# A recurrent mixer's instruction lists in another order, and the latent heads' key squares on another engine

## What is computed

```python
def wkv7_scan(r, w, k, v, a, b):
    # S_t = S_{t-1} diag(w_t) + (S_{t-1} a_t) b_t^T + v_t k_t^T ; y_t = S_t r_t
...
def rwkv7_mixer(r, k, v, dw, da, dg, w0, w2, a0, a2, g2, k_k, k_a, r_k, gn_w, gn_b):
    decay = jnp.exp(-jnp.exp(w_log))
    a = jax.nn.sigmoid((a0 + da @ a2).astype(f32))
    g = (jax.nn.sigmoid(dg) @ g2).astype(f32)
    kk = kk / jnp.maximum(jnp.sqrt(jnp.sum(kk * kk, axis=-1, keepdims=True)), 1e-12)
...
    y = wkv7_scan(rh, wh, kh, vh, -kk, kk * ah)
    y = ((y - mu) * lax.rsqrt(var + GN_EPS)).reshape(B, S, C) * gn_w + gn_b
    bonus = jnp.sum(rh * kh * r_k.astype(f32), axis=-1, keepdims=True) * vh
    return ((y + bonus.reshape(B, S, C)) * g).astype(r.dtype)
```

```python
    k_nope, v_mla = kv[..., :MLA_NOPE], kv[..., MLA_NOPE:]
    k = rms_norm_2(jnp.concatenate([k_nope, k_rope], axis=-1), g_mla_k)
    q = rms_norm_2(q, g_mla_q)
```

## Time and profile before

| what | us |
|---|---|
| median of 3 runs | 3263.35 (3263.17 to 3270.22) |
| the profiled execution | 3260.77 |
| its span, first to last instruction | 3258.7 |
| TensorE busy | 3138.0 (96%) |
| VectorE busy | 1681.2 (52%) |
| ScalarE busy | 1033.4 (32%) |
| GpSimd busy | 1968.5 (60%) |

### The profile page before, as it was taken

The page is one execution under the profiler, slowest core; times in us unless marked ns, Lnnn a source line. Parts: engine busy times, 40 slices in busy tenths (PEclk is TensorE's granted clock), DMA queues, the critical chain, the costliest instruction groups (busy, mean ns, idle before and its releaser), DMA issues.

```text
span 3258.7 us, 57483 instructions
## 1 busy us (share of the span) xinstructions
PE 3138.0 (96%) x20978; PEld 2472.2 (76%) x20978; DVE 1681.2 (52%) x2722; ACT 1033.4 (32%) x1860; POOL 1968.5 (60%) x2607
## 2 busy tenths in 40 slices
PE   7999999999999999999999999999999999999999
PEld 4767666678888886677778888877667778888887
DVE  4457777754553345525545644445551634555345
ACT  2153333321211113634443411123551536231112
POOL 4624333348688855254646888876336374898886
PEclk9999999999999999999999999999999999999999
DMA  5442111113233322022222333332113121333333
GB/s 213 143 161 60 42 41 47 41 54 117 69 97 97 99 74 71 27 66 65 65 66 72 91 97 97 97 92 83 40 35 90 45 84 46 94 94 97 97 97 97
DMA packets 70805, 265.42 MB, mean 81 GB/s; under 512 B 7744, under 2 KB 7872, under 8 KB 67520
## 3 DMA queue, kind: packets, MB, share of 16 engines
q1 hardware_dynamic: 68288, 257.59, 25.9%
q10 hardware_dynamic: 2304, 4.83, 0.4%
HBM read 260.29 MB, written 2.10 MB: 81 GB/s over the span
## 4 chain that ended last, share of the span: by engine, by line
PE 84%; DVE 9%; ACT 5%; issue 2%; DMA 1%; SPq 0%; DVEq 0%; ACTq 0%
PE psum_a L587 11%; PE psum_a L590 11%; PE psum_a L591 11%; PE psum_d L587 6%; PE psum_d L590 6%; PE psum_d L591 6%; PE psum_d L653 5%; PE psum_a L745 3%; PE psum_d L1119 2%; PE psum_d L848 2%; PE psum_a L775 2%; PE psum_a L779 2%; PE psum_a L778 2%; PE psum_a L616 1%; PE psum_a L619 1%
## 5 line engine op out<-in xcount | busy, mean ns | idle before, releaser
L3356 POOL TENSOR_TENSOR w_lo<-raw,w_hi 128x256 fp32r<-128x256 f32 x1736 | 1422.4, 850 | 36.2
L3350 POOL TENSOR_TENSOR mark<-mark 128x1 f32<-128x1 f32 x432 | 103.5, 240 | 1208.6 <-PE psum_a L587 610.8
L587 PE MATMUL psum_a<-h_hi,w_hi 128*128 128x512 f32 x1632 | 654.9, 401 | 6.2 <-ACT arena L1700 6.2
L591 PE MATMUL psum_a<-h_hi,w_lo 128*128 128x512 f32 x1632 | 636.9, 390 | 0.0
L590 PE MATMUL psum_a<-h_lo,w_hi 128*128 128x512 f32 x1632 | 636.9, 390 | 0.0
L3351 POOL TENSOR_SCALAR w_hi<-raw 128x1024 fp32r<-128x1024 f32 x434 | 460.9, 1062 | 33.1 <-DMA raw<-in_weights 33.1
L587 PEld LDWEIGHTS psum_a<-h_hi,w_hi 128*128 128x128 f32 x1632 | 306.6, 188 | 84.3 <-issue 11.0
L591 PEld LDWEIGHTS psum_a<-h_hi,w_lo 128*128 128x128 f32 x1632 | 306.8, 188 | 65.5
L590 PEld LDWEIGHTS psum_a<-h_lo,w_hi 128*128 128x128 f32 x1632 | 307.0, 188 | 61.5 <-issue 2.4
L587 PE MATMUL psum_d<-split,w_hi 128*128 128x512 f32 x848 | 329.9, 389 | 0.0
L590 PE MATMUL psum_d<-split,w_hi 128*128 128x512 f32 x848 | 329.9, 389 | 0.0
(11 more groups left out here) (374 smaller groups left out, 5272.9 us busy)
## 6 DMA issues: line engine op xcount, KB each, us to landing
raw<-in_weights SPq DMA_DIRECT2D x434, 512.0 KB, 3.6
plain<-in_ada SPq DMA_DIRECT2D x20, 1024.0 KB, 7.0
arena<-in_ada SPq DMA_DIRECT2D x4, 1024.0 KB, 16.8
x<-in_x SPq DMA_DIRECT2D x1, 2048.0 KB, 12.0
x<-in_x ACTq DMA_DIRECT2D x1, 2048.0 KB, 10.4
out<-x SPq DMA_DIRECT2D x8, 256.0 KB, 3.4
arena<-in_pe ACTq DMA_DIRECT2D x2, 512.0 KB, 3.8
const<-in_const ACTq DMA_DIRECT2D x1, 906.0 KB, 8.6
```

Of the source, the lines that this page charges most:

```text
L587: m = pe.eng.matmul(dst, wh, hi(t), start=t == 0, stop=False)
L591: m = pe.eng.matmul(dst, wl, hi(t), start=False, stop=t == k - 1)
L3350: eng.tensor_tensor(b.mark[:, 1:2], b.mark[:, 0:1], b.mark[:, 0:1], ALU.add)
L3356: m = eng.tensor_tensor(lo[:, part], b.raw[:, s, part], hi[:, part].bitcast(F32), ALU.subtract)
```

## The change

The mixer's lists:

- TensorE: `gate` is computed whole, ahead of the chain's maps (one tile of ring a in its turn, none taken ahead). The first of the pieces between the doublings has 4 weight tiles ahead of doubling 1 where it had 5, and 2 inside it where it had 1. The transposes of `R_KH` come behind the two products that follow them.
- ScalarE: the gate's Sigmoid comes ahead of the copies of the chain's outputs. `act_rwkv_decays` moves from doubling 2 to doubling 3, between the copy of the shifted input and `act_rwkv_length`.
- VectorE: the reciprocal of the group norm's deviation is two of 256 columns instead of one of 512, and it moves, with the first step of the norm behind it (`dve_rwkv_normed`), from behind `t_ready` to around the transitions, so ahead of the gate and the bonus. `dve_rwkv_mixed` moves from doubling 3 to behind `t_ready`. The steps of the next turn's inputs are dealt to other doublings: the scan (step 1) from the end of doubling 1 to that of 2, the first reciprocal from the end of 4 to the middle of 5 and the second from the middle of 5 to behind the maps.

The latent heads: the sums of the keys' squares are issued behind the first `uq` and ahead of the other three. ScalarE copies the upper half of a key bank and VectorE the lower half, then ScalarE squares all 128 rows from PSUM; VectorE's four squares go. The root of the key sums stands behind the first query.

```diff
 def pe_rwkv(pe, j, chain):
-    gate = PePieces(pe, "gate", 2 if chain else 0)
-    gate.part(4)
+    pe_features(pe, "a", "gate", H)
     if chain:
         chain.maps()
-    gate.part(4)
...
-    piece.part(5)
+    piece.part(4)
...
-        piece.part(1 if k == 1 else 2)
+        piece.part(2)
...
-    for src in (b.R_V, b.R_BH, b.R_KH):
-        turned = pe_turned(pe, [src[:, q * P:(q + 1) * P] for q in range(NQ)])
+    for src in (b.R_V, b.R_BH):
+        pe_turned(pe, [src[:, q * P:(q + 1) * P] for q in range(NQ)])
     pe_units(pe, "d", (B, R))
     maps = pe_units(pe, "d", (K, lambda v, row, out: AR[ROWS[row], 2 * v + out]), width=P)
+    turned = pe_turned(pe, [b.R_KH[:, q * P:(q + 1) * P] for q in range(NQ)])
 def pe_mla_heads(pe, half):
-        pe_features(pe, "a", "uk", of(b.s_hi, b.s_lo, 2), 1)
-    tiles = [pe_features(pe, "a", "uq", of(b.s_hi, b.s_lo), 2) for _ in range(4)]
-    pe.eng.wait_ge(pe.sem["key_sq"], pe.due("key_sq", 4))
-    pe_head_sums(pe, None, ones, [b.L_HQ[0:NOPE, 4 + n] for n in range(4)], b.L_KRQ[0:MQ])
+        b.key_banks.append(pe_features(pe, "a", "uk", of(b.s_hi, b.s_lo, 2), 1).ps)
+    tiles = [pe_features(pe, "a", "uq", of(b.s_hi, b.s_lo), 2)]
+    pe.eng.wait_ge(pe.sem["key_sq"], pe.due("key_sq", 2))
+    pe_head_sums(pe, None, ones, [b.L_HQ[r, 4 + n] for n in range(2) for r in ROWS], b.L_KRQ[0:MQ],
+                 [b.ones[r, 0:32] for n in range(2) for r in ROWS])
+    tiles += [pe_features(pe, "a", "uq", of(b.s_hi, b.s_lo), 2) for _ in range(3)]
 def act_mla_heads(a, l, half):
-        a.eng.activation(b.L_K[0:NOPE, 2 * n], ps[0:NOPE], ACT.Copy).then_inc(a.sem["key_raw"], a.up("key_raw"))
+        a.eng.sem_inc(a.sem["key_raw"], a.up("key_raw"))
+        a.eng.activation(b.L_K[0:NOPE, 2 * n + 1], ps[NOPE:2 * NOPE], ACT.Copy).then_inc(a.sem["act_step"], a.up("act_step"))
+        a.eng.wait_ge(a.sem["key_low"], a.due("key_low"))
...
+        a.eng.activation(b.L_HQ[:, 4 + n], ps, ACT.Square).then_inc(a.sem["free_a"], a.up("free_a"))
...
         act_twice(a, b.L_Q[:, n], b.L_HQ[:, n], MQ, b.col[:, 140:141])
-    act_head_root(a, b.L_ROWS[0][:, 1], P, MQ, "head_std")
+        if n == 0:
+            act_head_root(a, b.L_ROWS[0][:, 1], P, MQ, "head_std")
 def dve_mla_heads(v):
-    for n in range(4):
+    for n in range(2):
+        ps = b.key_banks.pop(0)
         v.eng.wait_ge(v.sem["key_raw"], v.due("key_raw"))
         v.eng.wait_ge(v.sem[v.last], v.own())
-        v.eng.tensor_tensor(b.L_HQ[0:NOPE, 4 + n], b.L_K[0:NOPE, n], b.L_K[0:NOPE, n], ALU.mult).then_inc(v.sem["key_sq"], v.up("key_sq"))
+        v.eng.tensor_copy(b.L_K[0:NOPE, 2 * n], ps[0:NOPE]).then_inc(v.sem["key_low"], v.up("key_low"))
```

More of the change, by code:

```diff
@@ L1242, in pe_rwkv, with pe_head_sums @@
     return PeChain(pe, maps, inverse, values)
-def pe_head_sums(pe, last, which, srcs, shared=None):
+def pe_head_sums(pe, last, which, srcs, shared=None, own=None):
     if last:
@@ L1251, in pe_head_sums @@
     for g, src in enumerate(srcs):
-        m = pe.eng.matmul(tl.ps[32 * g:32 * g + 32], which[0:src.shape[0]], src, start=True, stop=shared is None)
+        m = pe.eng.matmul(tl.ps[32 * g:32 * g + 32], own[g] if own else which[0:src.shape[0]], src, start=True,
+                          stop=shared is None)
     if shared is not None:
@@ L1728, in act_rwkv @@
         act_rwkv_inputs(a)
+    act_first_gate(a, b.x[:, j])
+    if j:
         act_rwkv_outputs(a)
-    act_first_gate(a, b.x[:, j])
     if more:
@@ L2456, in dve_rwkv_input @@
     if step == 4:
-        dve_shift(v, n + 1, b.R_R, j)
+        dve_shift_change(v, n + 1)
+    if step == 6:
+        dve_shift_mixed(v, n + 1, b.R_R, j)
     if step == 8:
@@ L2568, in dve_rwkv @@
     dve_rwkv_prepare(v, j)
+    if j >= 2:
+        dve_rwkv_inverse(v, 0)
     if j:
         dve_rwkv_transitions(v, j - 1)
+    if j >= 2:
+        dve_rwkv_inverse(v, 1)
+        dve_rwkv_normed(v, j - 2)
     v.eng.wait_ge(v.sem["gate_ready"], v.due("gate_ready"))
@@ L2590, in dve_rwkv @@
     if j >= 2:
-        dve_rwkv_normed(v, j - 2)
+        dve_rwkv_mixed(v, j - 2)
     for k in range(1, 6):
@@ L2614, in dve_rwkv @@
             dve_rwkv_carried(v, j)
-        if k in (1, 2, 4) and more:
-            dve_rwkv_input(v, j + 1, (1, 3, 0, 8)[k - 1])
-        if k == 3 and j >= 2:
-            dve_rwkv_mixed(v, j - 2)
+        if k in (2, 3, 4) and more:
+            dve_rwkv_input(v, j + 1, (1, 5, 6)[k - 2])
+        if k == 4 and more:
+            dve_rwkv_input(v, j + 1, 8)
     if j:
@@ L2622, in dve_rwkv @@
     if more:
+        dve_rwkv_input(v, j + 1, 10)
         dve_rwkv_input(v, j + 1, 9)
@@ L2635, in dve_rwkv_centered, with dve_rwkv_inverse @@
     v.eng.sem_inc(v.sem["centered"], v.up("centered"))
+def dve_rwkv_inverse(v, half):
+    std = v.b.R_STD[:, half * T // 2:(half + 1) * T // 2]
+    if half == 0:
+        v.eng.wait_ge(v.sem["gn_std"], v.due("gn_std"))
+    v.eng.wait_ge(v.sem[v.last], v.own())
+    v.eng.reciprocal(std, std).then_inc(v.sem["dve_step"], v.up("dve_step"))
 def dve_rwkv_normed(v, j):
     b = v.b
-    v.eng.wait_ge(v.sem["gn_std"], v.due("gn_std"))
-    v.eng.wait_ge(v.sem[v.last], v.own())
-    v.eng.reciprocal(b.R_STD, b.R_STD).then_inc(v.sem["dve_step"], v.up("dve_step"))
     v.eng.wait_ge(v.sem[v.last], v.own())
@@ L2791, in dve_shift, with dve_shift_change @@
 def dve_shift(v, n, dst, mu):
+    dve_shift_change(v, n)
+    dve_shift_mixed(v, n, dst, mu)
+def dve_shift_change(v, n):
     b = v.b
@@ L3201, in dve_program @@
             .then_inc(v.sem["act_lo"], v.up("act_lo"))
-    for step in (1, 2, 3, 5, 4, 8, 10, 9, 7):
+    for step in (1, 2, 3, 5, 4, 6, 8, 11, 10, 9, 7):
         dve_rwkv_input(v, 0, step)
```

13 lines of the change are left out of this document (8 added, 5 removed).

## The result

The changed kernel takes 3279.47 us (median of 6 runs, 3277.14 to 3283.37) against 3263.20 us (6 runs, 3261.52 to 3270.22): a ratio of 1.0052, 95% interval 1.0042 to 1.0062, so it is slower by 13.7 to 20.2 us. The forecast was 3268.0 us and no change; the measured time is 11.5 us above it and 0.5 us above the range's upper end. The profiled execution of the changed kernel took 3283.37 us, with a span of 3281.6 us; it is the slowest of the six.

What follows compares the result with a forecast made beforehand. TensorE, busy 96% of the span, was taken as the bound, with only its waits to win. Mixer -1 and heads +5.7 gave +4.7 us on 3263.35, so 3268.0 us and no measurable change; range 3257 to 3279 us.

Steps and rivals of the forecast that it cites:

- What bounds the kernel: Whole kernel: TensorE is busy for 96% of the span, so only its idle time can be won.
- The gate whole: Mixer's gate product: the 6.2 us wait ahead of it goes; fewer changes between big and small matmuls count 0.
- The doublings: Mixer's doublings: VectorE's steps dealt anew remove 20.7 us of TensorE's waits but for 1 us; bounds 0 to 5 left.
- The norm ahead of the bonus: Mixer, turns 2 to 7: A by B waits for VectorE's late bonus, 13.8 us in all; bounds 10 and 18.
- Exp behind the copy: Mixer, doubling 4, turns 0 to 6: N waits for ScalarE's late transpose, 12.1 us in all; bounds 8 and 15.
- The sum: Mixer's waits removed and added come to 0.0 us, taken as -1; with the heads' 5.7, +4.7 us in all.
- The heads: Latent heads, sums first: `uv` starts 1.65 us later in the first call; the four calls cost 5.7 us.
- A: Rival: the mixer wins what it removes, 26.9 us less 1, with the heads' 5.7 lost: 3243 us; chance 0.05.
- B: Rival: the heads' early root pays, each call ending up to 3 us sooner: 3250 us; chance 0.07.
- C: Rival: VectorE comes late to the mixer's transitions, 8.4 us more: 3276.4 us; chance 0.12.
- D: Rival: a 1.4 us drain after the table load delays doubling 4's N, 9.7 us more: 3277.7 us; chance 0.03.
- The signs: Mixer: old waits nearly gone, new ones of 2.4 and 1.6 us, turns as long; heads: waits for key and query squares.

Runs made afterwards that it cites:

- e8: The kernel before with only the gate product whole and the chain's maps behind it, ScalarE's list in matching order: 3254.42 us, ratio 0.9972.
- e7: The changed kernel with five unused matmuls on TensorE in the wait ahead of A by B, turns 2 to 6: 3270.88 us, ratio 1.0025 to before.
- e2: The kernel before with only the latent heads' part of the change: 3268.32 us, ratio 1.0019.
- e4: The changed kernel with ten unused matmuls on TensorE in the wait ahead of A by B, turns 2 to 6: 3282.00 us, ratio 1.0061 to before.
- e1: The changed kernel with the latent heads of the kernel before, so the mixer's part alone: 3271.36 us, ratio 1.0025 to before.
- e5: The changed kernel with the decays' table load and two Exp ahead of ScalarE's copy of the shifted input: 3265.36 us, ratio 1.0007 to before.
- e9: The kernel before with the key sums and root moved behind the first query product, squares still on VectorE: 3279.06 us, ratio 1.0047.
- e3: The changed kernel with the second half reciprocal and norm behind the inverse's first mask, mixing behind doubling 3: 3257.51 us, ratio 0.9985 to before.

## Why the prediction was wrong

**What bounds the kernel** held in part. TensorE is the engine that counts, but "only its idle time can be won" is not so: the busy time of the same matmuls moved too, by more than the idle time did.

**The gate whole**: the wait of 6.2 us went as said. e8 shows the part alone at 8.2 to 9.1 us with 6.6 us in its profile; I had counted the one change less between large and small products at 0, and busy time went down by 0.4 us. Where the timed runs have the rest isn't shown, and their interval (5.9 to 12.4) doesn't need one.

**The doublings**: 20.7 us went, 2.9 are left where I had 1.0 (three times 0.95 us at doubling 3's Z). Within the bounds. **Turn 1**, for which I took -1 us, took 0.7 us longer (57.3 for 56.6 us), nearly all of it busy time.

**The norm ahead of the bonus**: 14.4 us in turns 2 to 7 against 13.8 (2.64, 2.64, 2.30, 2.29, 2.29, 2.30 us). **Exp behind the copy**: 12.3 against 12.1 (2.76 in turn 0, 1.6 in each of the others). Both new waits were read rightly from rows without one run.

**The sum is the step that failed.** It reads -6.2 - 20.7 + 1.0 + 13.8 + 12.1 = 0, and as a sum of waits it is right: idle time in the mixer changed by +0.9 us. It puts the matmuls' own time at nothing, without a reason: it takes for granted that the same instructions cost the same on both sides. They don't: the waits that went were twelve of at most 1.8 us and others under 1 us, in a mixer whose granted clock was 1.00 on the whole, while the new ones are single stops of 2.3 to 2.8 us. Behind such a stop the clock falls in part of the cases, for about 1.5 us a time. Six falls more make most of the 10.5 us of busy time in the profiled execution, over 1 us of which stands at full clock; e7 measures 8.8 us for turns 2 to 6. With a term of 8 to 9 us the forecast of 3268.0 would have been 3276 to 3277. From the runs the 16.3 us come to 15.9: 0.9 of idle time in the mixer, 6.2 in the heads, 8.8 of clock, the last two with some 3 us either way.

**The heads**: forecast 5.7 us, measured 6.2 by e2's ratio and 6.4 by the shift in the profiles. `uv` was 1.64 us later for 1.65. A hit to the hundredth is luck in part: the sums waited 0.98 us in the first call where I had 1.3 and started 0.17 us sooner behind the key product, and from there to `uv` it took 7.84 us where I had 7.7. The lower copy took 0.68 us in all eight cases (taken: 0.69). The Trainium skill (SBUF — State Buffer, Who interferes with whom) says that a VectorE instruction with at most one SBUF input, outside the two-port modes, does not contend with GpSimd, and the trace agrees: GpSimd was at work beside the copies. My gains of 0.3 and 0.6 us in the second and fourth call came as 0.3 each: the four calls cost 1.7, 1.4, 1.8 and 1.4 us in the profiles, though TensorE waited 2.7 us for the key squares in these two. The last wait, for `heads_ready`, stayed as it was, as said.

**The rivals.** A and B did not happen. C gives 3276.4 us, near the measured time, but its mechanism isn't there: VectorE still idles 1.19 us ahead of the transitions in turn 3, and 11.5 us in the seven turns together. D isn't there either: the Exp starts at 463.96 and its table load ends at 462.67 + 1.28 = 463.95. The range had no case in which a stop costs more than its own length, and this is why its upper end fell short.

The signs that I had named were right on the mixer's waits, and wrong in the last: "a turn takes about as long as before". Turns 2 to 5 took 2.5, 1.8, 1.8 and 1.3 us longer (59.3, 60.1, 59.0 and 59.8 us against 56.8, 58.3, 57.1 and 58.5). A new wait of the same total as the old ones isn't a neutral exchange.

**What stays open**: which stops the clock answers to. Turn 6 of the changed kernel had a stop of 2.29 us and a clock of 1.00 in the same execution in which turn 5's stop of 2.29 us was followed by a fall, and e2 has a fall behind 1.71 us. The clock's share in the heads is read from single profiles and wasn't measured by filling the stops.

## What to carry to other kernels

Compare the busy time of the same matmuls before you trust a sum of waits: many short waits against one long one is not an even trade, since behind a long one the clock can fall, here for 1.5 us on top of 2.3 to 2.6. Where a long wait can't be removed, unused matmuls of about its own length win back the clock (e7), and fillings 1.9 us longer than the wait give it away again (e4). And before a step is put on an engine in front of another, look for the engine's idle time that ends on the same event anyway: the Exp cost 12.3 us behind the copy and nothing in front of it.

## What the runs showed of the hardware

- The same stop of 2.65 us, in the same place and behind the same instructions, was followed by a clock of 0.50 for some 3 us in one execution and by none in another. e1's nine runs span 9.4 us, and their mean clock sinks from 0.992 to 0.988 as the time rises.
- How often the clock fell behind a stop, over the profiles of the mixer: behind the 2.3 to 2.65 us at A by B in 11 of 20 cases (after 5 of 6, e5 5 of 6, e1 1 of 6, turn 7 of e4 and e7 none), behind the 2.8 us of turn 0 in 4 of 5 (not in e7), behind the 1.7 to 1.8 us at a doubling's Z in 2 of 12 (both in e2; none in before, e8 and e9), behind the 1.6 us at doubling 4's N in none of 30 (turns 1 to 6 of after, e1, e3, e4 and e7).
- A float matmul of 128x256 stands as two records of 0.23 us in the trace, and ten of them take 4.6 us.
- In the latent heads of e9 TensorE's waits grew by 8.6 us and the time by 15; in the profiles the other 8.6 us are busy time of the same instructions at a lower granted clock (0.90 for 0.95 in the second layer).
